# A mixture-of-experts layer, one core: the member count behind the first gate product, one constant matmul less, the second expert's product in two

## The reference

```python
def hierarchical_moe(hn, w_router_group, w_router_expert, w_gate, w_up, w_down):
    ...
    g_idx = jnp.argmax(g_logits, axis=-1)
    ...
    top_v, top_i = lax.top_k(e_sel, TOP_K_IN_GROUP)
    gates = g_w * jax.nn.softmax(top_v, axis=-1)
    ...
    def run_block(args):
        xb, e = args
        return (jax.nn.silu(xb @ w_gate[e]) * (xb @ w_up[e])) @ w_down[e]
    ...
    out = jnp.zeros((n, d), jnp.float32).at[row_token].add(ys.astype(jnp.float32) * row_gate[:, None])
```

## Time and profile before

| | |
|---|---|
| median of 3 runs | 980.68 us |
| the three runs | 980.67, 985.04, 980.68 us |
| the profiled execution | 981.12 us |
| its span | 979.4 us |
| busy, share of the span: TensorE matmuls | 794.4 us, 81% |
| VectorE | 474.4 us, 48% |
| ScalarE | 318.4 us, 33% |
| bytes moved by DMA | 286.72 MB, mean 293 GB/s |
| mean granted TensorE clock | 0.912 of full speed |

### The profile page before, as it was taken

One profiled execution on the slowest core, in us unless ns is written; L12 is line 12 of the kernel. 1 busy time (PEld: TensorE's weight loads), 2 busy tenths in 40 slices (PEclk: granted clock), 3 DMA queues, 4 the chain that ended last, 5 costly groups with the idle time before them and its releaser, 6 DMA issues.

```text
span 979.4 us, 15787 instructions
## 1 busy us (share of the span) xinstructions
PE 794.4 (81%) x6570; PEld 604.5 (62%) x6570; DVE 474.4 (48%) x825; ACT 318.4 (33%) x516; POOL 91.0 (9%) x112
## 2 busy tenths in 40 slices
PE   6999999999875673666657564678998999999996
PEld 6989898787533341342424333345977788888884
DVE  5855849555331220312203131226648687766775
ACT  6754355633100000000000000004585454444443
POOL 1029554200000000000000000000001000000000
PEclk9999999999977796977868787789999999999998
DMA  9984334578999999999999999999754546555101
GB/s 310 308 300 173 116 143 170 203 286 333 399 428 428 428 426 427 427 428 428 429 428 428 428 428 429 428 427 387 254 167 132 181 169 205 194 173 172 44 1 44
DMA packets 70756, 286.72 MB, mean 293 GB/s; under 512 B 11521, under 2 KB 36398, under 8 KB 58414
## 3 DMA queue, kind: packets, MB, share of 16 engines
q1 hardware_dynamic: 70386, 285.38, 74.1%
q10 hardware_dynamic: 316, 0.58, 0.2%
HBM read 284.90 MB, written 1.05 MB: 292 GB/s over the span
## 4 chain that ended last, share of the span: by engine, by line
PE 35%; DMA 35%; issue 21%; DVE 3%; POOL 3%; ACT 2%; SPq 0%; POOLq 0%; DVEq 0%; ACTq 0%
DMA down_a<-in_w_down_dram 27%; PE bank L571 12%; DMA pair_d<-in_w_up_dram 7%; PE bank L620 6%; PE bank L2155 5%; PE bank L599 3%; PE bank L2138 2%; PE bank L2106 1%; PE bank L2114 1%; PE bank L1971 1%; DVE act_p L518 1%; POOL seg_r L870 1%; PE bank L608 1%; ACT w_hi L546 1%; DMA res<-in_x_dram 1%
## 5 line engine op out<-in xcount | busy, mean ns | idle before, releaser
L556 DVE TENSOR_TENSOR w_lo<-ring,w_hi 128x1024 fp32r<-128x1024 f32 x137 | 177.3, 1294 | 118.7 <-ACT w_hi L546 118.2
L546 ACT ACTIVATE w_hi<-ring 128x1024 fp32r<-128x1024 f32 x138 | 146.1, 1059 | 187.2 <-PE bank L571 65.3
L571 PE MATMUL bank<-act_p,w_hi 128*128 128x256 f32 x736 | 139.5, 291 | 7.6 <-issue 7.6
L1677 DVE COPY y_e<-bank 32x256 f32<-32x256 f32 x64 | 27.2, 424 | 237.9 <-PE bank L2155 237.4
L571 PEld LDWEIGHTS bank<-act_p,w_hi 128*128 128x128 f32 x736 | 117.2, 195 | 10.4 <-issue 10.0
L587 PE MATMUL bank<-act_p,w_hi 128*128 128x512 f32 x352 | 122.2, 397 | 0.2 <-issue 0.2
L1141 ACT ACTIVATE y_e<-bank 32x256 f32<-32x256 f32 x64 | 23.9, 374 | 282.2 <-PE bank L2155 281.8
L571 PE MATMUL bank<-act_p,w_lo 128*128 128x256 f32 x368 | 105.2, 286 | 0.0
L620 PE MATMUL bank<-w_hi,act_q 128*128 128x512 f32 x304 | 95.3, 395 | 0.4 <-issue 0.4
L584 PE MATMUL bank<-act_p,w_lo 128*128 128x256 f32 x352 | 91.5, 280 | 0.0
L2155 PE MATMUL bank<-down_a,h_t 128*32 128x256 f32 x512 | 40.9, 474 | 58.8 <-DMA down_a<-in_w_down_dram 50.5
(11 more groups left out here) (378 smaller groups left out, 1047.0 us busy)
## 6 DMA issues: line engine op xcount, KB each, us to landing
ring<-in_w_up_dram SPq DMA_DIRECT2D x24, 2048.0 KB, 34.8
ring<-in_w_gate_dram SPq DMA_DIRECT2D x24, 2048.0 KB, 30.4
down_a<-in_w_down_dram SPq DMA_DIRECT2D x16, 2048.0 KB, 25.7
ring<-in_w_in_dram SPq DMA_DIRECT2D x15, 2048.0 KB, 19.0
down_b<-in_w_down_dram SPq DMA_DIRECT2D x15, 2048.0 KB, 25.9
ring<-in_w_ffn_in_dram SPq DMA_DIRECT2D x22, 1024.0 KB, 6.6
pair_d<-in_w_gate_dram SPq DMA_DIRECT2D x8, 2048.0 KB, 30.0
pair_d<-in_w_up_dram SPq DMA_DIRECT2D x8, 2048.0 KB, 34.5
```

The source lines that it names most:

```text
L546: nc.scalar.activation(parts(w_hi, g, view), view, ACT.Copy).then_inc(split_hi, 1)
L556: engine.tensor_tensor(parts(w_lo, g, view), view, h, ALU.subtract).then_inc(split_lo, 1)
L571: mm = nc.tensor.matmul(dst, parts(wt, g, grans[g][1])[:, k, :], a[:, x_part, k, :], start=(k == 0 and i == 0), stop=(k == KC - 1 and i == 2))
L1677: ins = nc.vector.tensor_copy(y_e[CAP * e:CAP * (e + 1), 256 * j:256 * (j + 1)], bank[2][CAP * j:CAP * (j + 1), 0:256])
```

## The change

Four edits, all at the start of the expert layer:

1. The two matmuls that fill `bank[7]` with the number of members move from ahead of `gather_first` to between expert 0's gate product and its up product.
2. `keep_running(2)` ahead of that gather becomes `keep_running(1)`.
3. Expert 1's product is made by `gate_up_apart`, in two halves, and stands before the turning of the gate matrix and not after it. It waits for the two halves of `x_t` one at a time.
4. SP waits for expert 1's own gate product (`gate_read` at 2) before it reloads that gate buffer, in place of its whole product.

```diff
         def load_expert(i, used, e, e_down, gate_first=False):
 
             if gate_first:
-                sp.wait_ge(gate_read, 1)
+                sp.wait_ge(gate_read, used)
                 load_half(i, 0, e)
             sp.wait_ge(gu_raw, used)
...
         for i in range(4):
-            load_expert(i, i + 1, 4 + i, 2 + i, i == 0)
+            load_expert(i, i + 1, 4 + i, 2 + i, i < 2)
...
         nc.tensor.matmul(bank[5][:, 0:NE], m_lt[:, :], rt[:, 4, 0, :], start=True, stop=True)
-        for dst, last in ((bank[5][:, NE:2 * NE], m_lt), (bank[7][:, 0:NE], ones)):
+
+        def members_in_front(dst, last):
             nc.tensor.matmul(dst, ones[:, :], rt[:, 4, 0, :], start=True, stop=False)
             nc.tensor.matmul(dst, last[:, :], rt[:, 4, 1, :], start=False, stop=True).then_inc(rank_raw, 1)
-        keep_running(2)
+
+        members_in_front(bank[5][:, NE:2 * NE], m_lt)
+        keep_running(1)
...
-        def gate_up_apart(e):
+        def gate_up_apart(e, xt):
             for n in range(2):
+                if e == 0 and n == 1:
+                    members_in_front(bank[7][:, 0:NE], ones)
                 pe.wait_ge(*pair_landed(e, n, 1))
                 gu = PAIR[e][:, n, :].rearrange("p (k n) -> p k n", k=KC)
                 for c in range(KC):
                     if c % 4 == 0:
-                        pe.wait_ge(xt_kept, c // 4 + 1)
+                        pe.wait_ge(xt_kept, xt + c // 4)
...
             else:
-                gate_up_apart(0)
+                gate_up_apart(0, 1)
                 pe.wait_ge(built, 2)
                 gather_first(CAP, P - CAP, bank[5:7], 0)
             if before is not None:
                 close_group(before)
+            if before is None:
+                gate_up_apart(1, 3)
             pe.wait_ge(built, 4 * k + 4)
             for b in range(TB):
                 mm = nc.tensor.transpose(bank[7][:, b * P:(b + 1) * P], gated[:, b, :], ident[:, :])
             mm.then_inc(gmat_raw, 1)
-            if before is None:
-                pe.wait_ge(xt_kept, 4)
-            gate_up_pe(k, s, 1)
+            if before is not None:
+                gate_up_pe(k, s, 1)
             down_pe(4 * k, 0, 2 * k + 1, before is None)
```

## The result

The changed kernel takes 986.4 us (median of 20 executions, 982.86 to 990.11), the kernel before on the same chip 982.02 us (20 executions, 980.6 to 986.8). The ratio is 1.0044, with a 95% interval of 1.0034 to 1.0054: **slower by 4.3 us**. The forecast was 979.4, and its range ended at 981.6. The profiled execution of the changed kernel took 989.14 us, span 987.4, where that of before had a span of 979.4.

The account below looks back on a forecast made before the run. The prediction took the stream of weight loads (bytes over rate) as the bound, so only its start could move. Terms -1.11 + 0.44 - 0.92 + 0.25 = -1.34 us gave 980.68 - 1.34 = 979.4 us, range 978.0 to 981.6.

Parts of the forecast that it names:

- the plateau's start moves with it: Expert layer's unbroken stretch of loads at about 428 GB/s: length is bytes over rate, start moves with the first down_a issue.
- The gather's start (-1.11): Ahead of expert 0's gather: without the members' pair and one constant, it waits only for onehot and starts 1.11 us earlier.
- The members in the product (+0.44): Between expert 0's gate and up product: the moved pair of member matmuls costs TensorE 0.44 us there.
- expert 1 (-0.92): Expert 1's product starts right behind the rest of the gather, without waiting for transposes and keep_rest: 0.92 us less.
- the transposes (+0.25): Turning of the gate matrix, now behind expert 1's product: comes back on the path with 0.25 us.
- The narrow form: Expert 1's product as 128 narrow records at 28.9 ns each, 3.70 us, costs no more than 64 wide ones.
- Rival 4: Expert 1's product: narrow records take as long as wide ones, 3.7 us more, 983.1 us; chance 1%.
- Late x_t, VectorE's cover: x_t's second half up to 0.15 us late for expert 1's product; VectorE's 0.35 us delay hidden, 0.2 us cover left.
- SP (0): SP's earlier wait on gate_read stands behind the wait for the first down product: costed at nothing.
- Rival 3: Expert 1's gate load goes out at 243.1 and fills the second hole in the load stream: 978.1 us; chance 3%.
- Rival 1: The stream of loads starts earlier by less, or part of the gain comes back later: 980.0 to 980.7; chance 16%.
- Rival 2: Half clock at the last products moves: loss over 1.3 us, chance 9%, up to 983.2; gain over 1 us, 5%.

Follow-up runs that it names:

- e1: The changed kernel plus a filling of 33 tiny constant matmuls (132 records) ahead of TensorE's loop; 984.52 us, ratio 1.0016.
- e2: The kernel before plus a filling of 31 tiny matmuls (124 records) ahead of the loop, nothing else changed; 986.95 us, ratio 1.0045.
- e4: The kernel before plus a filling of 64 tiny matmuls (256 records) ahead of the loop; 983.01 us, ratio 1.0018.
- e11: The kernel before plus a filling of 8 tiny matmuls (32 records) ahead of the loop; one execution, 984.59 us.
- after: The changed kernel with all four edits and no filling; 986.4 us, ratio 1.0044 to the kernel before.
- e3: The changed kernel with keep_running(2) back ahead of the gather and a filling of 32 tiny matmuls; 982.34 us, ratio 1.0007.
- e6: The kernel before with only expert 1's product in two ahead of the transposes and the SP edit, plus a filling of 32; ratio 1.0008.
- e7: The kernel before with only the members' count moved between gate and up product, both constants kept, no filling; ratio 1.0.
- e8: The kernel before with no constant matmul ahead of the gather (keep_running(0)) and a filling of 2; ratio 1.0022.

## Why the prediction was wrong

**The step that failed** is the one that carried the first issue through to the end: "the plateau's start moves with it", "all later issues 1.3 us earlier, to the last at 643.32". The length of the plateau was taken to be bytes over rate and untouched, since no edit acts in it. But the parts were counted as work and never as code. 125 more records ahead of the loop moved it to a place where its code does not stay loaded, by the rule above across eight blocks instead of seven, and the plateau became 3.6 us longer. e1, e2, e4 and e11 show it. No rival named it.

How much of the +4.3 us it is has two measures that agree roughly: e2 has it alone, +4.4 us (interval 2.7 to 6.1), and the changed kernel without it is e1, 1.0016 against 1.0044, 2.7 us less, though measured in another job and with an interval of its own of 0 to 3.1. The two later rounds in the profiles lie between, 3.0 to 3.5 us. The rest, about 1 us, would be the head, where the profile has +1.6 and the prediction -1.34; the medians are too coarse to show it.

**The gather's start (-1.11).** Right as a mechanism. The onehot ends last, at 229.86 + 0.51 = 230.37, and the gather begins at 230.42; its first weight load waited 0.8 us for it. From rank to gather 1.28 us were saved. Not foreseen: with one of the constants gone that bridged the time until the gather, the clock fell at the first products. Between after and e3, which differ at the head only by that matmul, the gather comes 1.62 and 2.39 us behind the rank matmul, and down_a's issue 22.0 and 20.8 us behind the table: 0.8 us were saved and 1.2 lost (0.2 of them ahead of the rank matmul, which no edit touches). The rows are in two profiles, so chance is in them too; six of seven against none of seven is what makes it more than a guess.

**The members in the product (+0.44), expert 1 (-0.92), the transposes (+0.25).** Three terms that were right in kind and wrong in size: +0.69, -0.71, +0.52 in e3. For expert 1's term half of the error is the reading of 241.94 named above, and half the switch. At full clock I estimate the change's head from these at -1.11 + 0.50 = -0.6 us, and not -1.34.

**The narrow form.** Right: 128 records in 3.70 us, 28.9 ns each. Rival 4 and the Trainium skill's rule beside it are out.

**Late x_t, VectorE's cover.** No wait in the middle of expert 1's product. The reduce came at 238.27, and not at 236.05, for the gate product was slow; keep_rest did not wait for it.

**SP (0).** Right. down_a at 249.78, expert 1's gate load at 250.16, behind it. Rival 3 did not happen.

**Rival 1 (eaten on the way)** is what is left once code and clock are put aside: e3, e6, e7. **Rival 2 (slower by the clock)** had the right engine and the wrong place. It looked at the last gate product. In the changed kernel's profile that one starts at 655.53 and takes 3.66 us at a clock of 1.00, where before it took 6.58, and nothing came of those 2.9 us: the chain runs through the last load, which landed at 670.15, and the down product behind it ran at 0.50. The fall that goes with the change is at the first products.

**The chances** (94% for no measurable change) rested on all cases lying within 0.5%. The measured 0.44% does lie within that bound, but 20 executions of each kernel tell it from nothing: the interval is 0.34% to 0.54%. The range missed it, for the range was built from the edits alone.

Open: the 18 packets are 0.29 MB, 0.7 us at 428 GB/s, and cost 3.0 to 3.5 us. In e11 the window from 421 to 660 moves 426 GB/s against 429 before, some 0.7% or 1.7 us over 239. A packet of q8 took 1.08 us on its DMA engine in after, one of the weights of the same 16 KB 0.62; if the 18 did not spread evenly over the 16 engines, the engine with most of them would end each load late. Whether it is that, or TensorE waiting for code, no view here tells, and it was not tried.

## What to carry to other kernels

When a change adds or removes instructions ahead of a loop, compare the number of instruction packets in the page's DMA section before anything else, and where it jumps, look for packets inside the loop. A filling of a few matmuls that moves the loop tells within one experiment whether a loss (or a gain) of some tenths of a per cent is the change's or its code's place. And a matmul of constants ahead of critical products must be tested by the clock of what follows it, not counted by its own duration.

## What the hardware showed that was not expected

- Whether TensorE keeps the code of a loop of 1752 records over its rounds depends on the loop's place: no packet in two rounds in eleven kernels, nine in each round in after, e2 and e11. The rule that fits the places is seven blocks of 256 records against eight.
- Eight small matmuls ahead of the loop made its second round of 117.47 us one of 118.99 (e11, one execution). Eleven kernels without the fetches agree on that round within 0.08 us.
- A switch between matmuls of the forms 128*128 and 128*32 costs TensorE some 0.1 us: 0.10 for one, 0.25 and 0.27 for two (e3).
- A busy TensorE lost half its clock: in 234 to 236 of e8 it is busy for 2.00 of 2.00 us at 0.50.
